# A fused two-block transformer kernel: the first retained head's steps begin six slots later

## What is computed

```
h = modulate(rmsnorm(x, norm_mix_g[l]), sh_m, sc_m)
proj = h @ w_in[l]
q, k, v, g_ret, b_cv, c_cv, u_cv, g_a, g_b = jnp.split(proj, split_pts, axis=-1)
q = rope(q.reshape(B, S, H, d), cos, sin)
k = rope(k.reshape(B, S, H, d), cos, sin) * (d ** -0.5)
y_ret = head_layernorm(retention_chunkwise(q, k, v, log_gamma)).reshape(B, S, RET_WIDTH)
y_a = (jax.nn.silu(g_ret) * y_ret) @ ret_w_out[l]
```

## Time and profile before

| | |
|---|---|
| median of 3 runs | 2520.94 us |
| the profiled execution | 2523.35 us, its span 2521.5 us |
| PE busy, weight load busy | 98%, 89% |
| VectorE, ScalarE, GpSimd busy | 72%, 47%, 19% |
| TensorE clock granted | 0.994 of full |
| retention beside its projections | about 1591 to 1816 us of the span |

### The profile page before, as it was taken

The page is one execution under the profiler, slowest core; times in us unless marked ns, Lnnn a source line. Parts: engine busy times, 40 slices in busy tenths (PEclk is TensorE's granted clock), DMA queues, the critical chain, the costliest instruction groups (busy, mean ns, idle before and its releaser), DMA issues.

```text
span 2521.5 us, 35427 instructions
## 1 busy us (share of the span) xinstructions
PE 2472.5 (98%) x13577; PEld 2236.7 (89%) x13593; DVE 1804.4 (72%) x3331; ACT 1172.8 (47%) x1969; POOL 484.4 (19%) x344
## 2 busy tenths in 40 slices
PE   8999999999999999999999999999999999999998
PEld 7788888899999998999999999788788888888887
DVE  7876678998998887688888887787786335533323
ACT  6555466367767777333333335444422223422222
POOL 3222164133322352333333310000000000000000
PEclk9999999999999999999999999999999999999999
DMA  4211345598988898999999983223375233232231
GB/s 167 69 60 43 117 156 166 193 329 320 346 311 302 313 396 323 382 373 367 373 370 363 366 296 110 76 84 97 106 267 182 93 100 109 76 101 100 92 102 42
DMA packets 191239, 519.15 MB, mean 206 GB/s; under 512 B 15896, under 2 KB 67096, under 8 KB 187872
## 3 DMA queue, kind: packets, MB, share of 16 engines
q1 hardware_dynamic: 154208, 382.66, 43.0%
q0 software_dynamic: 36864, 134.23, 14.7%
HBM read 464.34 MB, written 52.49 MB: 205 GB/s over the span
## 4 chain that ended last, share of the span: by engine, by line
PE 91%; DVE 6%; ACT 2%; issue 1%; DMA 1%; POOL 0%; DVEq 0%; SPq 0%; POOLq 0%; ACTq 0%
PE P L1247 28%; PE P L1249 27%; PE P L1248 27%; PE P L1592 2%; PE P L1254 1%; DVE wl L1704 1%; ACT wh L2338 1%; DVE D L1704 1%; POOL wl L2720 0%; PE P L1525 0%; PE P L1524 0%; PE P L1523 0%; PE P L1503 0%; PE P L1502 0%; PE P L1501 0%
## 5 line engine op out<-in xcount | busy, mean ns | idle before, releaser
L1247 PE MATMUL P<-XH,wh 128*128 128x512 f32 (+2 forms) x2272 | 850.9, 375 | 7.6 <-DVE wl L1704 5.1
L1249 PE MATMUL P<-XH,wl 128*128 128x512 f32 (+2 forms) x2272 | 825.4, 363 | 0.0
L1248 PE MATMUL P<-XL,wh 128*128 128x512 f32 (+2 forms) x2272 | 824.6, 363 | 0.0
L1704 DVE TENSOR_TENSOR wl<-raw,wh 128x1024 fp32r<-128x1024 f32 x418 | 507.5, 1222 | 54.0 <-ACT wh L2338 53.9
L2338 ACT ACTIVATE wh<-raw 128x1024 fp32r<-128x1024 f32 x458 | 480.7, 1053 | 133.6 <-PE P L1249 132.3
L1247 PEld LDWEIGHTS P<-XH,wh 128*128 128x128 f32 x2272 | 429.4, 189 | 53.4 <-DVE wl L1704 7.3
L1249 PEld LDWEIGHTS P<-XH,wl 128*128 128x128 f32 x2272 | 428.4, 189 | 47.7
L1248 PEld LDWEIGHTS P<-XL,wh 128*128 128x128 f32 x2272 | 429.2, 189 | 42.7 <-issue 1.9
L1247 PE MATMUL P<-AH,wh 128*128 128x384 f32 x1024 | 344.1, 336 | 1.8 <-DVE wl L1704 1.7
L1249 PE MATMUL P<-AH,wl 128*128 128x384 f32 x1024 | 342.7, 335 | 0.0
L1248 PE MATMUL P<-AL,wh 128*128 128x384 f32 x1024 | 342.7, 335 | 0.0
(11 more groups left out here) (326 smaller groups left out, 3342.6 us busy)
## 6 DMA issues: line engine op xcount, KB each, us to landing
raw<-wts SPq DMA_DIRECT2D x211, 512.0 KB
raw<-ut SPq DMA_DIRECT2D x128, 512.0 KB
raw<-vt SPq DMA_DIRECT2D x128, 512.0 KB
hdram<-HID SPq DMA_DIRECT2D x64, 384.0 KB
gdram<-GS SPq DMA_DIRECT2D x24, 1024.0 KB
GI<-gdram SPq DMA_DIRECT2D x16, 1536.0 KB, 13.1
HI<-hdram SPq DMA_DIRECT2D x32, 768.0 KB
AWC<-adat SPq DMA_DIRECT2D x64, 256.0 KB, 5.2
```

The source lines that it names most:

```text
L1247: e.matmul(bank, wh[:, w], H, start=start, stop=False)
L1248: e.matmul(bank, wh[:, w], L, start=False, stop=False)
L1249: return e.matmul(bank, wl[:, w], H, start=False, stop=stop)
L1704: return e.tensor_tensor(dst, a, b, op)
```

## The change

One pause is added in `retain()`, for head 0 alone, between the wait for the head and its first step. A pause of 6.0 takes six slots from the credit.

```diff
@@ -634,6 +634,8 @@
         for h in range(8):
             while h not in heads:
                 yield None
+            if h == 0:
+                yield 6.0
             for kb in range(4):
                 yield ("r_scores", h, kb)
                 if kb:
```

## The result

The changed kernel takes 2543.06 us, the median of 4 runs (2542.7 to 2544.21); the kernel before takes 2521.76 us beside it (4 runs, 2520.85 to 2524.21). The ratio is 1.0084 with a 95% interval of 1.0066 to 1.0101: 21 us **slower**, where 2542 was predicted. The profiled execution has 2543.1 us and a span of 2541.2, 19.7 more than that of the kernel before.

A forecast was written before the change was run, and what follows sets the result against it. PE, busy for 98% of the span, was taken as the bound. The terms -6.7 + 2.2 + 2.7 + 4.1 + 4.8 + 5.3 + 0.5 + 8.1 = +21.0 us on the median 2520.94 gave 2542 us, range 2529 to 2551.

The forecast's parts named there:

- Part 1: PE's 4.3 us gap before `r_scores(0, 0)` shrinks to 0.2 to 0.35 us and the clock stays up: -6.7 us.
- Part 2: Head 0: PE waits at `r_scores(0, 3)` for `r_decay(0, 1)`, now behind `rope(1, 0)` on VectorE: +2.2 us.
- Part 3: Heads 1 to 4: VectorE's supply outlasts PE's demand, so PE waits +2.7, +4.1, +4.8 and +5.3 us.
- Supply S: VectorE's time from the reduction of `r_turn(h)` to the end of `r_low(h, 3)`, counted as 24.4 us.
- The 0.5 us at head 5: Head 5, where `r_low` is again before `rope(6, 1)`: a remaining cost taken as +0.5 us.
- The waits before the roots: PE's 1.5 us before the root matmuls vanish for heads 2 to 4, return somewhat larger in 5 and 6: 0.
- Part 4: PE's clock drops behind the three waits of 4.1, 4.8 and 5.3 us, each with a 2.7 us tail: +8.1 us.
- A: Rival: PE's first gap is simply filled and VectorE has room for the rest; -6.7 us, 2514 us; chance 7%.
- B: Rival: PE's waits come but its clock holds; +12.9 us, 2534 us; chance 13%.
- C: Rival: it evens out, the waits of heads 2 to 4 being about half; 2521 to 2526 us; chance 6%.
- D: Rival: short waits drop PE's clock too, or a drop lasts longer; +26 us, 2547 us; chance 14%.

The follow-up runs named there:

- head 0 alone: The changed kernel with head 0's later pauses cut to 3.0, 1.6 and 0.4, so heads 1 to 7 keep their old slots; 2521.85 us, ratio 0.9994.
- both patterns: The kernel before with steps placed by slots, one pattern for head 0 (starting six slots late), another for heads 1 to 7; 2515.64 us, ratio 0.9974.
- moving one step back: The changed kernel with `r_low(h, 3)` given directly behind `r_decay(h, 3)`, without the pause of 3.5 between them; 2527.34 us, ratio 1.0014.
- 16 dummies: The changed kernel with 16 dummy 128x128 matmuls on PE ahead of `r_values` of heads 2, 3 and 4; 2536.19 us, ratio 1.0050.
- 28 dummies: The changed kernel with 28 dummy 128x128 matmuls on PE ahead of `r_values` of heads 2, 3 and 4; 2540.91 us, ratio 1.0073.
- the reciprocals early: The changed kernel with `r_factor(h)` directly behind `r_root(h)` and the pause of 4.4 moved behind it; 2540.63 us, ratio 1.0070.
- heads 1 on alone: The kernel before with a pause of 5.0 ahead of head 1 and none ahead of head 0; 2544.74 us, ratio 1.0082.
- a pause of 3: The changed kernel with `yield 3.0` in place of `yield 6.0`; 2529.77 us, ratio 1.0031.

## Why the prediction was right, point by point

- **Part 1**, -6.7 us. A wait of 0.20 us at slot 7 (predicted 0.2 to 0.35), full clock from 1592 to 1602 us. Right, and head 0 alone and both patterns show it again.
- **Part 2**, +2.2 us at `r_scores(0, 3)`, predicted to end at 1606.5: 2.27 us, ended at 1606.57. Right in time, but this wait dropped the clock as well in the profiled execution (1.7 us). The prediction had that only in a bound.
- **Part 3, supply and demand.** Supply S was 24.4 us; the rows of head 3 give 1708.97 + 0.28 - 1684.81 = 24.4 us, those of heads 2 and 4 the same. Waits: head 1 +2.7, measured 1.83 + 0.38 = 2.2; head 2 4.1 and 3.96; head 3 4.8 and 4.66; head 4 5.3 and 5.02. The order of steps as the cause is shown by moving one step back (14.0 us to 0.5). That the waits don't heal, since VectorE stands idle behind them, is in the rows at 1684.81 and 1718.93, and ends with head 5 as said. The 0.5 us at head 5 is not there. Nothing in the runs shows that term.
- **The waits before the roots**, taken as equal: 1.1 us after, 1.5 before.
- **Part 4, the clock**, +8.1 us by three tails of 2.7. Three tails of 1.6, 2.3 and 2.3 came, and a fourth of 1.7 in head 0: 7.9. That the sum fits is luck: each of the three was taken too long, and the one that was left out made up for it. That such a tail counts, and is not hidden by the next wait, was assumed there and is shown for heads 2 to 4 by the 16 dummies (5.9 of 6.2 us). It need not be so everywhere: with 28 dummies the clock fell behind the 1.84 us at the score of head 1, and the 0.38 us that PE waits at this head's values in the changed kernel are gone. The Trainium skill, "TensorE: Matmul & The Clock Gate", What's actually happening, says that the array idles at half rate and activity releases it. The trace agrees behind all three long waits (granted clock 0.50, then 1.00 again). For the waits of 2 us no row of the kernel before decided in advance.
- **The total.** Predicted +21.0, measured +21.3 between the medians and +19.7 between the profiled spans, of which rows explain 18.7. So the mechanism is right and the terms are 2.3 us too large together (head 1 by 0.5, heads 2 to 4 by 0.6, head 5 by 0.5, the roots by 0.4, gap and clock by 0.2 each); that the medians meet within 0.3 us is luck.
- **Rivals.** A, the gap simply filled (2514 us), fell. That both patterns reach 2515.6 does not give its price back: only 3.5 of their 6.6 us come with the gap, the rest with the pattern of the other heads. The Trainium skill, "Perfetto Trace Analysis", Optimization Strategy, says to find the gaps on the busiest engine and to let the dependency behind them start sooner or complete faster. Here the dependency stayed and its reader was moved, and that paid (2519.5 and 2515.6 us against 2543.1) only where the order on VectorE's queue was kept. B, the clock holds (2534 us), is what the version with 16 dummies comes near to, since its clock holds in heads 2 to 4: 2536.2, with the drop of 1.7 us in head 0 still in it. C, evening out, fell: S doesn't shrink. D, more clock, came in part: one of the two short waits dropped it.

## What to carry to other kernels

Where one written order serves all engines, a delay can cost nothing (two slots here) until a small step with a waiting reader falls behind a large one that nobody waits for; list, for each engine's queue, which steps change places, and compare the supply of the one with the demand of the other. Two engines that wait for each other in turn need not show on the page: here PE stayed at 98% and VectorE went from 72% to 71%, so neither busy share warned of it. A large wait on the bounding engine is worth filling only if the work drawn into it doesn't push the rest of the chain behind something else; here the same six slots cost 21 us in one arrangement and bring 6.6 us in another.

## What the runs showed of the hardware

- Waits of about 2 us drop PE's clock in some executions and not in others: the wait of 2.27 us at the same place had the clock at 0.84 from 1602 to 1613 us in the changed kernel and at 1.00 in the version with `r_low(h, 3)` early. Of the 15 waits of 1.8 to 2.9 us in this stretch in all profiled executions, 7 had a drop (1.84, 1.95, 2.13, 2.22, twice 2.27, and 2.89 us). Those of 3.8 to 5.0 us dropped it each time: 1 in the kernel before, 3 in the changed one, 3 with the reciprocals early, 4 with heads 1 on alone, 1 with a pause of 3.
- What a drop costs is not fixed by the wait's length: the 12 long waits lost 1.6 to 3.0 us of work each behind them, and waits of 3.96 and 3.98 us at the values of head 2 lost 1.6 us in the changed kernel and 2.9 with heads 1 on alone.
- A float32 matmul of 128x128 has two records and costs 0.22 us (56 records in 6.2 us). A count in a timeline's row is of records, not of matmuls.
